# Order and queues of the opening loads in a two-layer diffusion step, with the first modulation pair ahead of the input's transposes

## What is computed

```python
def modulation(cond, w_mod, b_mod):
    m = jax.nn.silu(cond) @ w_mod + b_mod          # (1024) @ (1024, 6144)
    return jnp.split(m[..., None, :], 6, axis=-1)

for l in range(2):
    mc = modulation(c_ctx, p["w_mod"], p["b_mod"])  # for the context tokens
    ml = modulation(c, p["w_mod"], p["b_mod"])      # for the latent tokens
    hc = xc * (1 + mc[1]) + mc[0]
    hl = xl * (1 + ml[1]) + ml[0]
    # layer 0: h @ w_in, then differential attention beside a Mamba-2 scan with
    # a depthwise convolution of 1024 channels; layer 1: multi-scale pooling
    x = layer_norm(ALPHA * x + m[2] * mixer(h), ln1_g, ln1_b)
    x = layer_norm(ALPHA * x + m[5] * sq_relu_mlp(x * (1 + m[4]) + m[3]), ln2_g, ln2_b)
```

## Time and profile before

| what | us |
|---|---|
| median of 3 runs | 1480.7 |
| lowest, highest | 1479.77, 1487.83 |
| the profiled execution, its own time | 1482.81 |
| span of its trace | 1481.0 |
| PE busy | 1408.0 (95% of the span) |
| DVE busy | 1040.0 (70%) |
| ACT busy | 543.2 (37%) |

### The profile page before, as it was taken

How to read it: one execution, slowest core, us unless ns; L and a number is a source line. 1 busy time by engine, 2 the same in 40 slices (tenths; PEclk the granted TensorE clock), 3 DMA queues, 4 the chain that set the end, 5 groups by cost and what they waited for, 6 DMA issues and landing times.

```text
span 1481.0 us, 22812 instructions
## 1 busy us (share of the span) xinstructions
PE 1408.0 (95%) x8806; PEld 1247.8 (84%) x8806; DVE 1040.0 (70%) x1645; ACT 543.2 (37%) x976; POOL 79.1 (5%) x146
## 2 busy tenths in 40 slices
PE   5999999899899999999999999979999999999996
PEld 3899998666688998998899879868899899889985
DVE  3694566576468976776676796756897677677678
ACT  3333352367435432332233244433543233223322
POOL 1300000011200000000000010000000000000001
PEclk9999999999999999999999999999999999999998
DMA  9701233586813322321231522651232232223141
GB/s 316 217 29 58 86 125 122 180 273 204 303 57 103 140 77 66 114 79 64 85 98 63 194 76 73 200 207 56 101 142 71 72 114 75 68 85 94 62 171 71
DMA packets 132300, 177.47 MB, mean 120 GB/s; under 512 B 4170, under 2 KB 104258, under 8 KB 131698
## 3 DMA queue, kind: packets, MB, share of 16 engines
q1 hardware_dynamic: 123250, 146.46, 30.6%
q0 software_dynamic: 7376, 26.76, 5.2%
q10 hardware_dynamic: 1584, 3.01, 0.5%
HBM read 166.94 MB, written 9.27 MB: 119 GB/s over the span
## 4 chain that ended last, share of the span: by engine, by line
PE 80%; DVE 8%; ACT 5%; DMA 3%; issue 2%; ACTq 0%; POOL 0%; SPq 0%; DVEq 0%; POOLq 0%
PE ps L765 39%; PE ps L1265 20%; PE ps L747 7%; PE ps L756 4%; PE ps L796 3%; DVE convT L1968 2%; DMA raw<-in_w_mod_l 2%; PE ps L1091 1%; ACT h_full L1669 1%; DVE wlo L1872 1%; ACT whi L1379 1%; ACT tmp L1669 1%; PE ps L1102 1%; DMA gate_parts<-modrow 1%; ACT e_att L1589 1%
## 5 line engine op out<-in xcount | busy, mean ns | idle before, releaser
L1379 ACT ACTIVATE whi<-raw 128x512 fp32r<-128x512 f32 (+2 forms) x186 | 175.4, 953 | 369.9 <-PE ps L765 307.2
L765 PE MATMUL ps<-whi,hid_hi 128*128 128x512 f32 x640 | 249.6, 390 | 0.0
L765 PE MATMUL ps<-wlo,hid_hi 128*128 128x512 f32 x640 | 249.2, 389 | 0.0
L765 PE MATMUL ps<-whi,hid_lo 128*128 128x512 f32 x640 | 249.0, 389 | 0.0
L1872 DVE TENSOR_TENSOR wlo<-raw,whi 128x512 fp32r<-128x512 f32 (+2 forms) x186 | 201.7, 1094 | 23.6 <-ACT whi L1379 20.1
L2301 DVE TENSOR_TENSOR acc<-acc,ps 128x512 f32<-128x512 f32 x120 | 80.2, 684 | 122.0 <-PE ps L765 122.0
L765 PE MATMUL ps<-whi,h_hi 128*128 128x256 f32 (+1 forms) x480 | 157.3, 328 | 5.8 <-DVE h_lo L2670 3.4
L765 PE MATMUL ps<-whi,h_lo 128*128 128x256 f32 (+1 forms) x480 | 152.9, 319 | 0.0
L765 PE MATMUL ps<-wlo,h_hi 128*128 128x256 f32 (+1 forms) x480 | 152.8, 318 | 0.0
L765 PEld LDWEIGHTS ps<-whi,hid_lo 128*128 128x128 f32 x640 | 120.2, 188 | 25.2
L765 PEld LDWEIGHTS ps<-whi,hid_hi 128*128 128x128 f32 x640 | 120.1, 188 | 25.2 <-DVE wlo L1872 0.8
(11 more groups left out here) (333 smaller groups left out, 2679.8 us busy)
## 6 DMA issues: line engine op xcount, KB each, us to landing
raw<-in_w_mod_l SPq DMA_DIRECT2D x39, 1024.0 KB, 5.2
raw<-in_w_up_l SPq DMA_DIRECT2D x32, 1024.0 KB, 5.6
raw<-in_w_down_l SPq DMA_DIRECT2D x32, 1024.0 KB, 5.0
raw<-in_w_in_l SPq DMA_DIRECT2D x12, 1024.0 KB, 5.3
raw_att<-in_w_mod_l SPq DMA_DIRECT2D x5, 1024.0 KB, 6.1
raw<-in_w_out_l SPq DMA_DIRECT2D x5, 1024.0 KB, 5.5
x_spill<-x_tok POOLq DMA_DIRECT2D x10, 512.0 KB, 2.9
x_tok<-x_spill POOLq DMA_DIRECT2D x10, 512.0 KB, 6.1
```

Source lines behind the costliest of these rows:

```text
L765: mm = pe.matmul(out, a_of(still, k), w_of(part, k), start=(first and k == 0 and part == 0 and still == 0), stop=(last and k == nk - 1 and ...
L1379: act.activation(ring_piece(whi, w, g), piece(w, g), ACT.Copy).then_inc(hi_done, 1)
```

## The change

The first two modulation blocks are issued first on SP, then the five tiles of x on the same queue, then the blocks from k = 2. `head` and the seven small vectors move from SP to ACT's queue, the six layer-norm vectors from ACT's queue to POOL's. Products 0 and 1 and their turns go ahead of x's transposes on TensorE, `mod_rows(0)`, `mod_rows(1)` ahead of the copies of x on ACT, and `mod_finish(0)`, `mod_finish(1)` ahead of the wait for them on DVE. DVE's silu goes ahead of the lambda products. The layer-norm vectors are turned in bank 4 in place of 7. `conv_in(0, (0, 1))` goes ahead of products 3 and turns 2 and 3; the wait for the layer-norm copy goes ahead of `conv_in(2, ...)`.

```diff
@@ SP
-            sp.dma_start(head[:], A["t_head"]).then_inc(ld_head, 16)
-            sp.dma_start(vec_rows[0:8, 0, :], ...)          # c, and six more small vectors
-            ...
-            k = 0
+            load(0)
+            load(1)
+            for t in range(NT):
+                src = x_sample[0, t * P:(t + 1) * P, :] if t < LAT else x_prompt[0]
+                sp.dma_start(x[:, t, :], src).then_inc(x_ld[t], 16)
+            k = 2
@@ POOL, behind the four lamv loads
+            for n, name in enumerate(("ln1_g_l0", "ln1_b_l0", "ln2_g_l0", "ln2_b_l0", "ln1_g_l1", "ln1_b_l1")):
+                pool.dma_start(vec_rows[8 * n:8 * n + 8, 1, :], ...).then_inc(ld_ln, 16)
@@ TensorE
             pe.transpose(bank(6, 128, 224), vec_rows[0:96, 2, :], ident[0:96, 0:96]).then_inc(vec_tr, 1)
+            pe.wait_ge(vec_cp, 1)
+            pe.wait_ge(c_ok, 1)
+            mod_product(0)
+            mod_product(1)
+            mod_turn(0)
+            mod_turn(1)
             for t in range(NT):
...
-            pe.transpose(bank(7, 0, 48), vec_rows[0:48, 1, :], ident[0:48, 0:48]).then_inc(vec_tr, 1)
-            pe.wait_ge(c_ok, 1)
-            pe.wait_ge(vec_cp, 2)
+            pe.transpose(bank(4, 0, 48), vec_rows[0:48, 1, :], ident[0:48, 0:48]).then_inc(vec_tr, 1)
...
-            mod_product(0)
-            mod_product(1)
-            mod_turn(0)
-            mod_turn(1)
             mod_product(2)
+            pe.wait_ge(xT_ev, NT)
+            conv_in(0, (0, 1))
             mod_product(3)
             mod_turn(2)
             mod_turn(3)
-            conv_in(0, (0, 1))
             conv_in(1, (0, 1))
@@ ACT
-            for t in range(NT): act.dma_start(x[:, t, :], src)      # and the six layer-norm vectors
+            act.dma_start(head[:], A["t_head"]).then_inc(ld_head, 16)
+            act.dma_start(vec_rows[0:8, 0, :], ...)                 # c, and six more small vectors
...
             act.activation(thc[:, 0, :], vecT[:, 0:16], ACT.Tanh, scale=0.5).then_inc(small_act, 1)
+            mod_rows(0)
+            mod_rows(1)
             act.wait_ge(lam_s, 2)
@@ DVE: silu ahead of the lambda products, then
+            mod_finish(0)
+            mod_finish(1)
             dve.wait_ge(vec_tr, 2)
```

More of the change, by code:

```diff
@@ L573, in _ @@
                 pool.dma_start(lamv[:, n, :], A[name].partition_broadcast(P)).then_inc(ld_lam, 16)
+            for n, name in enumerate(("ln1_g_l0", "ln1_b_l0", "ln2_g_l0", "ln2_b_l0", "ln1_g_l1", "ln1_b_l1")):
+                pool.dma_start(vec_rows[8 * n:8 * n + 8, 1, :], A[name].rearrange("(k p) -> k p", p=P)).then_inc(ld_ln, 16)
             steps = [0]
@@ L858, in _ @@
             mod_product(6)
+            pe.wait_ge(vec_cp, 2)
             conv_in(2, (0, 1, 2, 3))
@@ L1410, in six @@
                 return ps[:, b * 512:b * 512 + cols]
[L1412 to L1416, removed]
+            act.dma_start(head[:], A["t_head"]).then_inc(ld_head, 16)
+            act.dma_start(vec_rows[0:8, 0, :], A["c"].rearrange("a (k p) -> (a k) p", p=P)).then_inc(ld_vec, 16)
+            act.dma_start(vec_rows[8:16, 0, :], A["c_ctx"].rearrange("(k p) -> k p", p=P)).then_inc(ld_vec, 16)
+            act.dma_start(vec_rows[16:56, 0, :], A["conv_w_l0"].rearrange("j (k p) -> (j k) p", p=P)).then_inc(ld_vec, 16)
+            act.dma_start(vec_rows[56:64, 0, :], A["conv_b_l0"].rearrange("(k p) -> k p", p=P)).then_inc(ld_vec, 16)
+            act.dma_start(vec_rows[64:72, 0, :], A["pool_scale_l1"].rearrange("(k p) -> k p", p=P)).then_inc(ld_vec, 16)
+            for l in range(2):
+                act.dma_start(vec_rows[48 * l:48 * l + 48, 2, :],
+                              A[f"b_mod_l{l}"].rearrange("(k p) -> k p", p=P)).then_inc(ld_vec, 16)
             act.wait_ge(vec_cp, 1)
             act.activation(thc[:, 0, :], vecT[:, 0:16], ACT.Tanh, scale=0.5).then_inc(small_act, 1)
+            mod_rows(0)
+            mod_rows(1)
             act.wait_ge(lam_s, 2)
@@ L1425, in _ @@
             for q in range(4):
-                mod_rows(2 * q)
-                mod_rows(2 * q + 1)
+                if q >= 1:
+                    mod_rows(2 * q)
+                    mod_rows(2 * q + 1)
                 for f in (2 * q, 2 * q + 1):
@@ L1912, in _ @@
             mark(dve.tensor_scalar(scales, scales, 1.0, None, ALU.add))
-            dve.wait_ge(ld_lam, 64)
             dve.wait_ge(vec_cp, 1)
[L1915 to L1919, removed]
             dve.wait_ge(small_act, 1)
@@ L1928, in _ @@
             mark(dve.tensor_scalar(vecT[:, 16:64], vecT[:, 16:64], 0.5, None, ALU.mult))
+            dve.wait_ge(ld_lam, 64)
+            for n in range(2):
+                mark(dve.tensor_tensor(lamv[:, 2 * n, :], lamv[:, 2 * n, :], lamv[:, 2 * n + 1, :], ALU.mult))
+            settle()
+            for n in range(2):
+                dve.reduce_sum(lsum[:, n:n + 1], lamv[:, 2 * n, :], AX.X).then_inc(lam_s, 1)
+            mod_finish(0)
+            mod_finish(1)
             dve.wait_ge(vec_tr, 2)
-            dve.tensor_copy(lns[:, 0:48], bank(7, 0, 48)).then_inc(vec_cp, 1)
+            dve.tensor_copy(lns[:, 0:48], bank(4, 0, 48)).then_inc(vec_cp, 1)
             dve.wait_ge(small_act, 2)
@@ L1941, in _ @@
             for q in range(4):
-                mod_finish(2 * q)
-                mod_finish(2 * q + 1)
+                if q >= 1:
+                    mod_finish(2 * q)
+                    mod_finish(2 * q + 1)
                 dve.wait_ge(mod_out, 2 * q + 2)
```

## The result

The changed kernel takes 1.0044 times the time of the kernel before (95% interval 1.0026 to 1.0062; medians 1491.3 and 1484.45 us), and in a second lot, on one chip with the kernel before, 1.0063 (1.0044 to 1.0082). That is 6.5 and 9.3 us slower, where I had forecast 0.6 us faster. The medians are of six executions each, and the kernel before has 1484.45 in them where the three of the forecast had 1480.7, so the ratio and not the absolute time is what to compare. One execution of each kernel, of 2013 and of 4932 us, was slow and is left out of the ratio. The profiled execution has a span of 1488.5 us in place of 1481.0, 7.5 more, and took 1490.28.

The account below looks back on a forecast made before the run. PE was taken as busy 95% of the span, its opening waiting on vectors, transposes and, behind them, DMA. M gained 3.2 us, conv_in gave back most: T -0.6 us, 1480.7 to 1480.1 us, range 1476.5 to 1484.5.

Parts of the forecast that it names:

- the landing of the small vectors: Opening loads on ACT's queue: vectors land at 7.2 us instead of 12.2, bounded between 6.3 and 12.2.
- M: Moment DVE can begin to modulate: forecast 22.1 us in place of 25.34, 3.2 us earlier.
- V: First TensorE instruction, when the small vectors are there: forecast 7.2 us, 12.32 before.
- pair 0: Products 0 and 1 with their turns, ahead of x's transposes: forecast at the half clock, from 8.8 to 15.1 us.
- The transposes: x's 40 transposes on TensorE behind products 0 and 1: mostly at the fast rate, 5.9 us, ending at 21.0.
- the rival on their half clock: x's transposes run at the half clock, 7.9 us: T 40.4, a loss of 1.4 us, 1482.1 us; chance 0.22.
- conv_in ahead of product 3: Six pairs of matmuls, 3.2 us, delay product 3 to 31.7 us and give back most of the gain at M.
- T: Start of the projection of tiles 2 and 3: forecast 38.4 us beside 38.96 before.
- the case with more kept: Rival: the clock is up again early or stays up, T 36.4, capped by block 7, 1477.3 to 1478.1 us; chance 0.25.
- T goes to the end one for one: Chain behind T has no slack, so whatever is won or lost there reaches the end: forecast -0.6 us.
- C: DVE's first convolution: forecast 0.6 us before its old 60.07.
- The one on vectors that land no earlier: Rival: DMA engines, not the queue, hold the vectors up at 12.2; T 42.8, 3.8 us lost, 1484.5 us; chance 0.12.

Follow-up runs that it names:

- e1: Changed kernel with POOL's broadcast and layer-norm loads held until the small vectors land, and the lambda work moved behind the first pairs; ratio 1.0031 to the kernel before.
- f1: Kernel before with POOL's four broadcast loads held until the small vectors land, and the lambda work behind the pairs; ratio 0.9985.
- h1: e1 with SP's blocks also held until the small vectors land, so these load alone; slow by design, one run, vectors at 5.28 us.
- g1: Changed kernel with the broadcast loads held as in e1 and conv_in(0, (0, 1)) put back behind turn 3; ratio 1.0004 to the kernel before.
- g2: f1 with 12 and 14 unread identity transposes ahead of products 2 and 3 to keep TensorE busy; ratio 0.9990 to the kernel before.
- i1: g2 with the lambda work one pair further back and POOL's small loads issued behind product 3 instead of product 7; ratio 0.9981 to the kernel before.
- e4: Changed kernel with conv_in(0, (0, 1)) put back behind turn 3, the rest of the change kept; ratio 1.0028 to the kernel before.
- the second trace: Changed kernel run once more without edits, on one chip with the kernel before; ratio 1.0063.
- e2: Kernel before with only the change's order and queues of the opening loads, all engines computing in the old order; ratio 1.0024.
- e3: Kernel before with only conv_in(0, (0, 1)) moved ahead of product 3 and its turns; ratio 1.0020.
- b2: Kernel before run once more without edits; projection of tiles 2 and 3 at 38.86 us, DVE's first convolution at 59.95 us.

## Why the prediction was wrong

**The step that failed is the landing of the small vectors.** I bounded it between 6.3 and 12.2 us and took 7.2; it was 13.97, outside these bounds, and that is 6.8 of the 7.8 us by which M missed (29.92 against 22.1). The price rested on an argument for which no row spoke, that a vector's packet waits for a shorter packet now. The row that spoke against it was in front of me: 234 GB/s in the stretch in which the vectors land. I wrote that this stretch stays, and then let the vectors pass it by. e1 and f1 show that the broadcasts in it cost the vectors some 2 to 4 us, and h1 that other traffic beside them costs nearly another 5. A smaller part of the same step failed too, that eight issues take about as long on ACT as on SP: the last ended at 5.23 us and not at 4.28. The Trainium skill's warning (DMA: Bandwidth & Descriptors, Issuing engines are not separate DMA queues), that DMAs interleave on the same engines whoever issues them, is what the runs show. From its rule of turns between queues (same page, Queues, rings and completion order) I drew an early landing beside short rows; no run bears this out: 10.08 and 9.99 beside 1 KB rows, 10.18 and 9.49 beside 4 KB rows. Counted from the start of the last issue it is 5.5 us in e1 and g1 and 5.9 and 6.1 in g2 and i1, so that short rows and the other queue together gave some 0.5 us at most, where I had put 5.

**The price of the new order was hidden in the same step.** My sum had M 14.9 us behind V; in the kernel before it is 13.0. I compared two absolute times and did not see that for equal vectors the new order loses 1.9 us. The traces have 15.0 on the mean of six with the new order (13.7 to 16.0, h1 left out) and 12.7 on that of seven with the old one (12.1 to 13.3). The terms, first trace against first trace: silu's way from the vectors to `cpad` stands ahead of all work (1.78 instead of 0.31 us), pair 0 runs at the half clock (6.3 instead of 4.1), and the transposes, partly at the full clock, give 0.8 back; the rest is 0.1. Before, x's transposes covered silu and were done while the clock was low.

**The transposes** took 7.0 us, not 5.9: by their duration the clock had not risen after pair 0's 6.3 us of broken work. This is part of the rival on their half clock (7.9), and it is the rest of M's miss. It is not so in every execution: in e1 and e4, with the same order, product 1 took 1.53 and 1.51 us, between the two levels, the transposes ran at the full clock, and M - V is 13.7 instead of 15.4 to 16.0.

**conv_in ahead of product 3: right, and a loss by itself.** From M to T I had 16.3 us; the traces have 15.9 to 17.1 with this order (mean 16.5) and 13.5 to 14.5 with the old one and no filler (mean 14.1). Its steps came out one by one: 6.4 us from M to the end of the low half (29.92 to 36.32), 3.3 for the 12 matmuls, 3.6 from turn 3's end to that of `hlo` (42.14 to 45.76). Product 3 took 1.07 and not 1.5, as the clock rose just ahead of it; in the second trace it took 1.94, which is a good part of the 1.1 us by which T - M is longer there.

**The other landings.** Nothing waited for block 3; issued at 8.26, it took 17.4 us and so was there at 25.7, where I had 25.1. By 13.5 us 164 x 5.3 + 231 x 5.1 + 399 x 3.1 = 3.28 MB had moved in place of 3.50, which accounts for that. Block 1 came at 13.0 and not at 10.8, when about 3.1 MB had moved and not my 2.4, so bytes issued behind it went beside it; x's last tile came at 19.7 and not at 18.0. None of these held TensorE up, as the vectors were later still; with vectors at 7.2 us block 1 would have held product 1, forecast at 11.3. Block 7's landing as the cap of a gain, which I named for the case with more kept, is what i1 runs into (38.04 where I had 37.55).

**T goes to the end one for one: right** as far as the convolution (21.1 us in 12 of 14 traces). Behind it the stretch from C to the end is 1418 to 1428 us in the traces, with no relation to T, so that a single time can't be set against T to the microsecond; the ratios can, within their intervals.

**The rivals.** The one on vectors that land no earlier, to which I gave 0.12, had the right cause. It had T = 42.8 for vectors at 12.2 and transposes of 5.3; with 1.8 for the vectors at 13.97 and 1.7 for transposes of 7.0 it has 46.3, beside 45.81 measured. It was cut off at the old landing, and so was the range: that the landing could become later than before was never priced.

**Adding up,** means of the traces: the loads 1.8 us (V), pair 0 ahead of the transposes 2.3 (M - V), the place of `conv_in` 2.4 (T - M), together 6.5, beside the measured 6.5 and 9.3. e2, e3 and g1, which have one part each, leave 3.6, 3.0 and (against f1) 2.8 by their ratios, with intervals of 2 to 3 us either way.

## What to carry to other kernels

Price a change of order as the difference between the two orders from the same event, not as a new absolute time beside an old one: an optimistic landing otherwise pays for a worse order. A small load that gates the start was held up by what was in flight beside it, and moving it to another queue did not help; what helped was keeping loads that nobody needs yet out of its way. Work put forward in an in-order engine to fill a wait must be ready before the work that it displaces; `conv_in` waited for a longer chain than product 3 did, and moved that wait to everything behind it.

## What the runs showed of the hardware

- Eight small loads (0.18 MB in all) land at 5.3 us alone, at 9.5 to 10.2 beside a stream of 361 to 394 GB/s, and at 11.4 to 14.4 where such a stream has beside it four broadcast loads of 32 KB from POOL.
- With these four early, all queues together move 227 to 252 GB/s from 5.3 to 10.4 us (eight traces) instead of 361 to 394 (five with them held); from 231 to 361 and from 234 to 394 that is 0.65 and 0.8 MB for 0.13 MB of their own. Issued at about 10 us instead of 1.3 they cost 0.4 us in f1 and 0.7 in g2. Issued at 5.4, as SP's stream begins, they come with a slow stretch again (h1, 239 GB/s from 10.4 to 13.5). Why they are so slow beside the start of the stream was not settled.
- The landing differs by 1 us and more between executions of the same loads (11.40 and 12.33; 12.92 and 14.43), and M moves with it; T does so only where no block of the stream is waited for in between (38.96 and 38.86 for M 0.9 us apart).
- In f1 TensorE idled from 21.9 to 23.8 us, behind work with gaps of 0.6 us, and the granted clock fell to the 1.2 GHz level while product 2 ran; it was 0.50 from 25 to 28.9. In b2 1.6 us without work ahead of product 2 were followed by the same fall. 26 transposes that nobody reads kept it at 2.4 GHz and were worth 1.9 us at T.
